# Two sums of an S5 step moved from VectorE to GpSimd, and the scan placed two places later

## The chip, the core and the metric

The kernel runs on one core of a Trainium2 chip. Its engines are TensorE (PE in the profile, its weight loads PEld), VectorE (DVE), ScalarE (ACT), GpSimd (POOL) and SyncE (SP); 16 DMA engines move the data. Each engine has its own list of instructions and runs it in order, and the lists meet in semaphores. The metric is the device time of one execution in microseconds; lower is better.

## The reference

A two-layer decoder trunk over 256 tokens of 1024 channels in float32. Layer 0: RMSNorm and a mixer of dilated attention and a gating unit. Layer 1: RMSNorm, then an S5 layer and a sigmoid GLU. Behind each mixer stands a PEER layer: for each token and each of 8 heads, 16 of 16384 experts are chosen, and an expert is a row u and a row v of 1024 channels each:

```python
act = jax.nn.gelu(jnp.einsum('td,tkd->tk', xbb, u_tab[ib]))
return jnp.einsum('tk,tkd->td', gb * act, v_tab[ib])
```

The S5 layer is a complex diagonal recurrence along time. For each state, with input x (real part xr, imaginary xi) and a fixed complex factor a of size `dec` and angle `th`, it computes s[k] = a s[k-1] + x[k], and the output is the real part of a product with c, plus a skip.

## The kernel before

**The frame.** The 256 tokens are two halves t = 0, 1 of 128 (one on each partition). Two layers by two halves by 8 heads by 16 experts make 512 *places* g. For each place GpSimd issues one gather (L463) that brings u and v rows for 128 tokens, 1 MB, into one of nine ring buffers. VectorE takes the dot of u with the token (`dot_product`, L1324, 128x1024, both operands in SBUF). ScalarE makes gelu, weight and a diagonal matrix (`weights`, L661 to L667), and TensorE multiplies the diagonal by v (`expert`, L920), which adds to a sum in PSUM. The gather of place g waits for the expert matmuls of place g - 9, since it takes their buffer.

**The rest of the work** hangs between the places. A table WORK, written by hand in `between()`, names for each place what else is done there. Each engine goes through the same table and takes the stages that it has a function for. On VectorE the stages of a place come before its dot; on ScalarE before its weights; on TensorE before the expert matmuls of the place ahead. So a stage at place p waits on each engine for that engine's work of the places before.

**S5.** The first half's S5 layer runs in the places behind 128, the second's in those behind 256. Each goes through eight steps c = 0 to 7 of 128 channels (512 states, 4 columns of 128 times per part), nine places apart: slot = 11 + 9c. To keep the recurrence real, the input is turned by the angle of its time, scanned with the real factor, and turned back. The stages of step (t, c):

- s5_turns (ScalarE, L591 and L593, at slot + 3 of the step before): the turns for each time, and `whole`, the rounded turns
- s5_frac (VectorE, L1186, at slot + 4 of the step before): waits for `whole`, leaves the fraction
- s5_tables (ScalarE, at slot + 6 of the step before): cosine and sine tables
- s5_in (TensorE): the input in PSUM
- s5_rot (VectorE, L1213 and L1214, slot + 1): input by cosine and by sine, 128x1024 each, from PSUM and a table; then w_ok
- s5_add (VectorE, L1218 and L1219, slot + 2): the two sums, 128x512 each; in the second half also the start value (L1223)
- s5_scan (VectorE, L1231 twice, slot + 3), and in the first half a copy of the last column (L1235)
- s5_cmat (ScalarE, L629 and L631, slot + 4)
- s5_back (VectorE, L1240 and L1242, slot + 5): two products 128x1024
- s5_out (TensorE, L882 and L886, slot + 6): waits for both products; then yc_done, for which the next s5_rot waits

The choice of the experts of later heads (`route_...`) also runs on VectorE in between, mostly with operations of one input.

Of the kernel before, what the change touches and what calls it, by code (L numbers as in the profile page):

```python
# [19 lines left out]
ALU = mybir.AluOpType  # L20
# [9 lines left out]
KC = D // P  # L30
# [3 lines left out]
PH, NK, TOPK = 8, 128, 16  # L34
EXPERTS = NK * NK
GROUPS = 2 * T * PH
RING = 9
AHEAD = 16
PACE = 1
DIAGS = 16  # L40
# [54 lines left out]
def between():  # L95

    work = {n: {} for n in range(GROUPS)}

    def at(n, slot, *stages):
        work[n + slot // TOPK].setdefault(slot % TOPK, []).extend(stages)  # L100

    def query(n, slot, phase, b):
        at(n, slot, ("q_mm", phase, b, 0, 3))
        at(n, slot + 1, ("q_mm", phase, b, 3, 6))
        at(n, slot + 2, ("q_mm", phase, b, 6, 8))
        at(n, slot + 3, ("q_in", phase, b))
        at(n, slot + 4, ("q_turn", phase, b))
        at(n, slot + 6, ("q_copy", phase, b))
        at(n, slot + 7, ("q_score", phase, b))
        at(n, slot + 9, ("q_keep", phase, b))  # L110

    def norm(n, slot, m):
        for i, name in enumerate(("norm_sq", "norm_ms", "norm_sd", "norm_h", "norm_T", "hT_copy")):
            if m < 8 or i < 4:
                at(n, slot + i, (name, m))

    def mix_norm(n, slot, m):
        for i, name in enumerate(("norm_sq", "norm_ms", "norm_sd", "norm_r", "norm_d", "norm_T", "hT_copy")):
            at(n, slot + i, (name, m))

    def product(n, slot, name, *which):
        at(n, slot, (name, *which, 0, 3))
        at(n, slot + 1, (name, *which, 3, 6))
        at(n, slot + 2, (name, *which, 6, 8))

    def attention(n, slot, a):
        for i, name in enumerate(("att_scores", "att_max", "att_exp", "att_den", "att_pT", "att_pT_copy", "att_o")):
            at(n, slot + i, (name, a))

    at(0, 0, ("z_out", 6), ("z", 7, 0, 8), ("z", 8, 0, 8), ("z", 9, 0, 8), ("z_out", 7), ("z_out", 8), ("z_out", 9))  # L130
    at(0, 2, ("qk_turn", 1))
    at(0, 3, ("qkT_copy", 1))
    query(0, 6, 0, 1)
    at(1, 1, ("sgu_var", 1))
    at(1, 2, ("sgu_sd", 1))
    at(1, 3, ("sgu_norm", 1))
    at(1, 4, ("sgu_mm", 1))
    at(1, 5, ("sgu_gate", 1))
    attention(1, 6, 1)
    query(1, 13, 0, 2)  # L140
    attention(2, 6, 2)
    at(2, 14, ("mix", 1))
    at(2, 15, ("mix_T", 1))
    at(3, 0, ("mixT_copy", 1))
    product(3, 1, "w_mm", 1, 0)
    at(3, 4, ("w_sum", 1, 0))
    product(3, 4, "w_mm", 1, 1)
    at(3, 7, ("w_sum", 1, 1))
    norm(3, 8, 3)
    query(3, 14, 0, 3)  # L150
    query(4, 4, 1, 3)
    for slot, *names in ((78, "s5_dt"), (79, "s5_th"), (80, "s5_dec"), (81, "s5_n"), (82, "s5_trig"), (84, "s5_k"),
                         (86, "s5_b0"), (90, "s5_b1"), (106, "s5_bT"), (108, "s5_bT_copy")):
        at(0, slot, (names[0],))
    query(0, 76, 1, 0)
    query(0, 84, 1, 1)
    query(0, 92, 1, 2)
    for t in range(T):
        g = PH * (t + 1)
        at(g, 2, ("y_sum", 2 + 2 * t))  # L160
        mix_norm(g, 3, 4 + 2 * t)
        at(g, 3, ("s5_turns", t, 0))
        at(g, 4, ("s5_frac", t, 0))
        at(g, 6, ("s5_tables", t, 0))
        for c in range(KC):
            slot = 11 + 9 * c
            at(g, slot - 1 if c == 0 else slot - 6, ("s5_in", t, c))
            at(g, slot, ("s5_decay", t, c))
            at(g, slot + 1, ("s5_rot", t, c))
            at(g, slot + 2, ("s5_add", t, c))  # L170
            at(g, slot + 3, ("s5_scan", t, c))
            at(g, slot + 4, ("s5_cmat", t, c))
            at(g, slot + 5, ("s5_back", t, c))
            if c + 1 < KC:
                at(g, slot + 3, ("s5_turns", t, c + 1))
                at(g, slot + 4, ("s5_frac", t, c + 1))
                at(g, slot + 6, ("s5_tables", t, c + 1))
            at(g, slot + 6, ("s5_out", t, c))
            if c % 4 == 3:
                at(g, slot + 8, ("s5_gelu", t, c // 4))  # L180
        for b in range(2):
            at(g, 82 + 2 * b, ("glu_mm", t, b, 0, 4))
            at(g, 83 + 2 * b, ("glu_mm", t, b, 4, 8), ("gate_T", t, b))
            at(g, 86 + 2 * b, ("glu_sig", t, b))
            at(g, 87 + 2 * b, ("glu_sum", t, b))
        norm(g, 90, 5 + 2 * t)
        for b in range(4):
            query(g, 96 + 6 * b, 2 + t, b)
    at(24, 2, ("y_sum", 6))
    norm(24, 3, 8)  # L190
    for n, slot in ROUTE_AT.items():
        for name, i in ROUTE:
            at(0, slot + i, (name, n))
    return work


WORK = between()

LAST = [("y_sum", 7), ("norm_sq", 9), ("norm_ms", 9), ("norm_sd", 9), ("norm_h", 9)]
# [6 lines left out]
def trunk(nc, x_in, vecs, cols_in, cst_in, w_in, sgu_g, sgu_wT, sgu_bT, w_out, s5_par, s5_b, s5_c, glu_w, wq, skT, uv_tab,  # L206
          out):
    with ExitStack() as ctx:
# [3 lines left out]
        def sem(name):  # L212
            return ctx.enter_context(nc.semaphore(name))
# [46 lines left out]
        def part(start, size, pattern="p (a s) -> p a s", **dims):  # L260
# [43 lines left out]
        by_cos, by_sin = (part(5888 + 1024 * v, 1024, "p (r j s) -> p r j s", r=2, j=4) for v in range(2))  # L304
# [14 lines left out]
        ld_vec, ld_col, ld_row = sem("ld_vec"), sem("ld_col"), sem("ld_row")  # L319
        got = [sem(f"got{b}") for b in range(RING)]  # L320

        r_ok, rd_ok, sn_done, dt5_ok, dd_ok = (sem(n) for n in ("r_ok", "rd_ok", "sn_done", "dt5_ok", "dd_ok"))
        sq_done, ms_done, sd_done, h_done, nT_done, hT_act, hT_dve, x_done, w_used = (sem(n) for n in (
            "sq_done", "ms_done", "sd_done", "h_done", "nT_done", "hT_act", "hT_dve", "x_done", "w_used"))

# [122 lines left out]
        @block.gpsimd  # L448
        def _(pool):
            pool.wait_ge(ld_sgu, 48)  # L450
            sg3 = sgw[:, :].rearrange("p (h i) -> p h i", h=8)
            nc.gpsimd.affine_select(out=sg3, in_=sg3, pattern=[[0, 8], [1, P]], compare_op=ALU.is_ge, fill=0.0, base=0,
                                    channel_multiplier=-1).then_inc(sgm_ok, 1)

            for g in range(GROUPS * TOPK):
                n, s = g // TOPK, g % TOPK
                if s == 0:
                    pool.wait_ge(idx_ok, n + 1)
                if g < RING and g % 2 == 0:
                    pool.wait_ge(z_done, 6 + g // 2)  # L460
                if g >= RING:
                    pool.wait_ge(v_done, g - RING + 1)
                nc.gpsimd.indirect_dma_start(  # L463
                    out=ring[g % RING], out_offset=None, in_=uv_tab,
                    in_offset=bass.IndirectOffsetOnAxis(ap=idx[n % AHEAD][:, s:s + 1], axis=0)).then_inc(got[g % RING], 16)

# [478 lines left out]
        def _(dve):  # L945
            V = nc.vector
# [267 lines left out]
                V.tensor_tensor(by_sin, x4, sin, ALU.mult).then_inc(w_ok, 1)  # L1214
                dve.drain()

            def s5_add(t, c):
                V.tensor_tensor(by_cos[:, 0, :, :], by_cos[:, 0, :, :], by_sin[:, 1, :, :], ALU.add)  # L1218
                V.tensor_tensor(by_cos[:, 1, :, :], by_cos[:, 1, :, :], by_sin[:, 0, :, :], ALU.subtract)  # L1219
                dve.drain()  # L1220
                if t == 1:

                    V.tensor_tensor(by_cos[:, :, :, 0], by_cos[:, :, :, 0], z_last[:, :, 4 * c:4 * c + 4], ALU.add)  # L1223
                    dve.drain()

            def s5_scan(t, c):

                dve.wait_ge(dt5_ok, KC * t + c + 1)
                for r in range(2):
                    w = by_cos[:, r, :, :].rearrange("p j s -> p (j s)")  # L1230
                    ins = V.tensor_tensor_scan(w, decay.rearrange("p j s -> p (j s)"), w, 0.0, ALU.mult, ALU.add)  # L1231
                ins.then_inc(sn_done, 1)
                dve.drain()
                if t == 0:
                    V.tensor_copy(z_last[:, :, 4 * c:4 * c + 4], by_cos[:, :, :, P - 1])  # L1235
# [83 lines left out]
            def dot_product(g):  # L1319
# [8 lines left out]
                         att_max=att_max, att_den=att_den, sgu_var=sgu_var, sgu_norm=sgu_norm, sgu_gate=sgu_gate, mix=mix,  # L1328
                         mixT_copy=mixT_copy, w_sum=w_sum, q_copy=q_copy, y_sum=y_sum, s5_n=s5_n, s5_k=s5_k,
                         s5_b0=s5_b0, s5_b1=s5_b1, s5_rot=s5_rot,  # L1330
                         s5_frac=s5_frac, s5_add=s5_add, s5_scan=s5_scan, s5_back=s5_back, glu_sum=glu_sum, norm_r=norm_r)
            stage |= dict(route_keys=route_keys, route_pairs=route_pairs, route_best=route_best, route_index=route_index,
                          route_gate=route_gate)

            def run(stages):
                for name, *args in stages:
                    if stage.get(name):
                        stage[name](*args)
# [82 lines left out]
```

## Time and profile before

| | |
|---|---|
| median of 3 runs | 1553.53 us (1551.04 to 1553.55) |
| the profiled execution, its own time | 1553.37 us |
| its span, first to last instruction | 1551.6 us |
| VectorE, ScalarE, GpSimd busy | 1111.5, 770.2, 589.4 us |
| TensorE matmuls, mean granted clock | 1097.8 us, 0.781 |
| gathers | 512, 84.8% of the DMA engines' span |

The 1.8 us between span and time lie around the first and the last instruction. Busy shares are means over stages with different limits, so they don't say what bounds a stage; the windows and the waits of a stretch do. A wait of an engine counts only where that engine sets the end.

### The profile page before, as it was taken

The page shows a single profiled execution, that of the slowest core. Times are in us where ns is not written, and L with a number is a line of the kernel's source. Part 1 is how long each engine was busy: PE and PEld are TensorE (multiplying, and loading weights), DVE is VectorE, ACT ScalarE, POOL GpSimd, SP SyncE. Part 2 cuts the span into 40 slices and gives each one's busy share as a digit, 9 for nine tenths or more (in the row PEclk, how much of TensorE's full clock was granted, in tenths as well). Part 3 has the DMA queues.
Part 4 walks back from the last instruction along what each step waited for, and adds up shares of the span by engine and source line. Part 5 has one row for each costly group of instructions (what it writes and reads, how often), then busy time and mean ns, then how long its engine had stood idle before and what let it go on. Part 6 is the DMA issues. An engine that isn't in the chain of part 4 may idle for free.

```text
span 1551.6 us, 19133 instructions
## 1 busy us (share of the span) xinstructions
PE 1097.8 (71%) x5920; PEld 348.4 (22%) x5920; DVE 1111.5 (72%) x2533; ACT 770.2 (50%) x2120; POOL 589.4 (38%) x517
## 2 busy tenths in 40 slices
PE   7997678866765666679866575656878666666665
PEld 3542222322211212223221121212323111111110
DVE  2356887479787899985477799999456866666554
ACT  2315554445456667764334666766334644444433
POOL 0024343323443354554334345344432443434430
PEclk9998689878966776879988567686998777676675
DMA  9569999999999998999999999999999999999995
GB/s 358 179 234 413 420 405 418 414 415 408 415 421 421 354 374 358 410 421 415 412 413 414 403 357 369 355 363 406 380 416 415 415 422 421 421 421 421 421 422 234
DMA packets 105418, 603.39 MB, mean 389 GB/s; under 512 B 9314, under 2 KB 9442, under 8 KB 39780
## 3 DMA queue, kind: packets, MB, share of 16 engines
q0 software_dynamic: 73728, 536.90, 84.8%
q1 hardware_dynamic: 31588, 65.26, 11.3%
q8 instruction: 47, 0.77, 0.2%
q14 instruction: 55, 0.45, 0.1%
HBM read 601.08 MB, written 1.05 MB: 388 GB/s over the span
## 4 chain that ended last, share of the span: by engine, by line
DMA 32%; DVE 31%; PE 22%; ACT 7%; issue 3%; DVEq 3%; ACTq 1%; POOL 1%; SPq 0%; POOLq 0%
DMA rings<-in_uv_tab_dram,idx 24%; DVE rings L1324 11%; PE ps L715 9%; PE ps L920 8%; DMA wst<-in_wq_dram 7%; DVE mem L1231 2%; PE ps L908 2%; DVE dgs L1324 2%; ACT dgs L667 1%; DVE mem L1213 1%; ACT wgt L664 1%; DMA rings<-in_w_in_dram 1%; DVE mem L1242 1%; ACT L661 1%; DVE mem L1240 1%
## 5 line engine op out<-in xcount | busy, mean ns | idle before, releaser
L920 PE MATMUL ps<-rings,dgs 64*64 64x512 f32 x3648 | 638.0, 804 | 343.3 <-ACT dgs L667 342.6
L463 POOL DMA_INDIRECT rings<-in_uv_tab_dram,idx x456 | 521.7, 1144 | 804.3 <-PE ps L920 687.8
L1324 DVE CUSTOM_DVE_ANT_0 rings<-rings,h 128x1024 f32<-128x1024 f32 x456 | 550.7, 1224 | 210.8 <-DMA rings<-in_uv_tab_dram,idx 197.7
L661 ACT ACTIVATE gel<-dots 128x1 f32<-128x1 f32 x512 | 102.1, 199 | 522.2 <-DVE dots L1324 518.5
L920 PEld LDWEIGHTS ps<-rings,dgs 64*64 64x64 f32 x3648 | 128.3, 163 | 783.4 <-ACT dgs L667 682.3
L667 ACT ACTIVATE dgs<-cst,wgt 128x128 f32<-128x128 f32 x512 | 205.6, 402 | 36.3 <-issue 1.5
L715 PE MATMUL ps<-wst,hT 128*128 128x512 f32 x320 | 168.0, 666 | 37.1 <-DMA wst<-in_wq_dram 20.5
L664 ACT ACTIVATE wgt<-gel,share 128x1 f32<-128x1 f32 x512 | 150.8, 295 | 35.5 <-issue 0.3
L920 PE MATMUL ps<-dgs 64*64 64x512 f32 x448 | 80.2, 795 | 53.2 <-ACT dgs L667 53.1
L463 POOL DMA_INDIRECT dgs<-in_uv_tab_dram,idx x56 | 65.9, 1176 | 88.3 <-PE ps L920 74.8
L715 PEld LDWEIGHTS ps<-wst,hT 128*128 128x128 f32 x320 | 63.4, 212 | 138.1 <-issue 134.9
L1324 DVE CUSTOM_DVE_ANT_0 dgs<-dgs,h 128x1024 f32<-128x1024 f32 x56 | 68.5, 1223 | 26.5 <-DMA dgs<-in_uv_tab_dram,idx 24.5
L661 ACT ACT_TABLE_LOAD x56 | 71.8, 1283 | 3.8 <-DVE dots L1324 2.2
L715 PE MATMUL ps<-rings,hT 128*128 128x512 f32 x128 | 59.0, 611 | 3.7 <-DMA rings<-in_w_in_dram 2.8
L1324 DVE DVE_READ_ACCUMULATOR2_ANT dots<- 128x1 f32 x512 | 42.6, 83 | 0.0
L648 ACT ACT_TABLE_LOAD x31 | 39.8, 1283 | 0.8
L920 PEld LDWEIGHTS ps<-dgs 64*64 64x64 f32 x448 | 14.2, 156 | 106.9 <-ACT dgs L667 101.2
L1231 DVE TENSOR_TENSOR_SCAN mem<-mem 128x512 f32<-128x512 f32 x32 | 37.4, 1210 | 0.0
L556 ACT ACTIVATE mem<-ps 128x512 f32<-128x512 f32 x16 | 9.5, 594 | 53.6 <-PE ps L715 53.6
L715 PEld LDWEIGHTS ps<-rings,hT 128*128 128x128 f32 x128 | 24.4, 197 | 33.2 <-issue 33.1
L1108 DVE COPY mem<-ps 128x512 f32<-128x512 f32 x16 | 11.0, 689 | 27.4 <-PE ps L707 27.4
L908 PE MATMUL ps<-wst,hT 128*128 128x512 f32 x64 | 29.6, 605 | 0.0
(192 smaller groups left out, 991.2 us busy)
## 6 DMA issues: line engine op xcount, KB each, us to landing
wst<-in_wq_dram SPq DMA_DIRECT2D x15, 2048.0 KB, 28.2
wst<-in_w_out_dram SPq DMA_DIRECT2D x4, 2048.0 KB, 22.8
wst<-in_glu_w_dram SPq DMA_DIRECT2D x4, 2048.0 KB, 31.7
rings<-in_uv_tab_dram,idx POOLq DMA_INDIRECT x456, 15.7
rings<-in_w_in_dram SPq DMA_DIRECT2D x3, 2048.0 KB, 16.7
rings<-in_w_in_dram SPq DMA_DIRECT2D x2, 1024.0 KB, 7.5
dgs<-in_w_in_dram SPq DMA_DIRECT2D x1, 2048.0 KB, 19.4
vec<-in_vecs_dram SPq DMA_DIRECT2D x3, 512.0 KB, 17.2
```

What stands on the lines that cost most here:

```text
L463: nc.gpsimd.indirect_dma_start(out=ring[g % RING], out_offset=None, in_=uv_tab, in_offset=bass.IndirectOffsetOnAxis(ap=idx[n % AHEAD][:, s ...
L648: A.activation(gexp[n % 2][:, :], cs[n % 2][:, :], ACT.Exp, bias=ncs[n % 2], accum_out=gsum[n % 2]).then_inc(exp_ok, 1)
L661: A.activation(gel[i][:, every], dots[i][:, every], ACT.Gelu_apprx_tanh)
L664: A.activation(wgt[i][:, c], gel[i][:, c], ACT.Copy, scale=share[n % AHEAD][:, c])
L667: A.activation(diag[:, (g + k) % DIAGS, :], ident, ACT.Copy, scale=wgt[i][:, c]).then_inc(diag_ok, 1)
L715: ins = PE.matmul(ps[:, bank, :], lhs[:, k, :], rhs[:, k, :], start=(k == 0), stop=(k == KC - 1))
L908: ins = PE.matmul(ps[:, 2 + b, :], hTs[t][:, k, :], wst[:, w % 2, k, :], start=False, stop=(k == KC - 1))
L920: ins = PE.matmul(ps[64 * b:64 * b + 64, 4 + 2 * t + half, :], diag[rows, g % DIAGS, rows], ring[g % RING][rows, D + b * BANK:D + (b + 1) ...
L1213: V.tensor_tensor(by_cos, x4, cos, ALU.mult)
L1231: ins = V.tensor_tensor_scan(w, decay.rearrange("p j s -> p (j s)"), w, 0.0, ALU.mult, ALU.add)
L1240: V.tensor_tensor(by_sin, by_cos, sin, ALU.mult).then_inc(d_ok, 1)
L1324: V.tensor_tensor_reduce(out=u, in0=u, in1=h[:, t, :], scale=1.0, scalar=0.0, op0=ALU.mult, op1=ALU.add, accum_out=dots[n % 2][:, s:s + 1] ...
```

## The change

The two sums of s5_add leave VectorE and go to GpSimd, between its gathers. GpSimd goes through the same table six places behind its gathers: ahead of the gather of place g it does the stages of place g - 6. It waits for w_ok ahead of the sums and raises add_ok behind them. On VectorE s5_scan waits for add_ok, and the addition of the start value moves into it. In the table the scan goes from slot + 3 to slot + 5 and s5_back from slot + 5 to slot + 6; s5_add stays at slot + 2, which counts for GpSimd alone.

```diff
+POOL_LAG = 6
...
-            at(g, slot + 3, ("s5_scan", t, c))
+            at(g, slot + 5, ("s5_scan", t, c))
             at(g, slot + 4, ("s5_cmat", t, c))
-            at(g, slot + 5, ("s5_back", t, c))
+            at(g, slot + 6, ("s5_back", t, c))
...
+            def s5_add(t, c):
+
+                pool.wait_ge(w_ok, KC * t + c + 1)
+                nc.gpsimd.tensor_tensor(by_cos[:, 0, :, :], by_cos[:, 0, :, :], by_sin[:, 1, :, :], ALU.add)
+                nc.gpsimd.tensor_tensor(by_cos[:, 1, :, :], by_cos[:, 1, :, :], by_sin[:, 0, :, :],
+                                        ALU.subtract).then_inc(add_ok, 1)
+
+            stage = dict(s5_add=s5_add)
+
+            def run(stages):
+                for name, *args in stages:
+                    if name in stage:
+                        stage[name](*args)
+
             for g in range(GROUPS * TOPK):
                 n, s = g // TOPK, g % TOPK
+                if g >= POOL_LAG:
+                    run(WORK[(g - POOL_LAG) // TOPK].get((g - POOL_LAG) % TOPK, []))
                 if s == 0:
                     pool.wait_ge(idx_ok, n + 1)
...
-            def s5_add(t, c):
-                V.tensor_tensor(by_cos[:, 0, :, :], by_cos[:, 0, :, :], by_sin[:, 1, :, :], ALU.add)
-                V.tensor_tensor(by_cos[:, 1, :, :], by_cos[:, 1, :, :], by_sin[:, 0, :, :], ALU.subtract)
-                dve.drain()
+            def s5_scan(t, c):
+
+                dve.wait_ge(add_ok, KC * t + c + 1)
                 if t == 1:
 
                     V.tensor_tensor(by_cos[:, :, :, 0], by_cos[:, :, :, 0], z_last[:, :, 4 * c:4 * c + 4], ALU.add)
                     dve.drain()
-
-            def s5_scan(t, c):
-
                 dve.wait_ge(dt5_ok, KC * t + c + 1)
```

## Rows read from the trace of the kernel before

**Rows 1.** The page: engines, and slices of VectorE, GpSimd and DMA.
```profile
PE 1097.8 (71%) x5920; PEld 348.4 (22%) x5920; DVE 1111.5 (72%) x2533; ACT 770.2 (50%) x2120; POOL 589.4 (38%) x517
...
DVE  2356887479787899985477799999456866666554
POOL 0024343323443354554334345344432443434430
...
GB/s 358 179 234 413 420 405 418 414 415 408 415 421 421 354 374 358 410 421 415 412 413 414 403 357 369 355 363 406 380 416 415 415 422 421 421 421 421 421 422 234
```
**Rows 2.** Windows: PE, PEld, DVE, ACT, POOL busy; clock, DMA share, GB/s.
```profile
520.00:640.00 120.00, 74.44 (x586) 24.33 (x586) 114.36 (x217) 82.12 (x227) 55.35 (x42) 0.73 0.93 363
640.00:680.00 40.00, 27.54 (x244) 9.52 (x244) 36.39 (x55) 31.08 (x91) 21.89 (x18) 0.81 1.01 421
...
880.00:1080.00 200.00, 125.86 (x911) 38.41 (x912) 189.49 (x377) 132.72 (x365) 92.38 (x71) 0.71 0.94 369
...
1120.00:1500.00 380.00, 260.90 (x1284) 58.45 (x1280) 249.57 (x593) 162.18 (x484) 154.42 (x147) 0.74 1.01 419
```
**Rows 3.** VectorE's waits in 880 to 1080 us: total, times, longest.
```profile
DVE tiny L1315 <- ACT gexp L648: 1.2, 1, 1.2
DVE cand L1304 <- issue: 0.4, 1, 0.4
```
**Rows 4.** VectorE's waits in 1120 to 1500 us.
```profile
DVE rings L1324 <- DMA rings<-in_uv_tab_dram,idx: 99.5, 81, 2.0
DVE dgs L1324 <- DMA dgs<-in_uv_tab_dram,idx: 16.4, 12, 2.5
```
**Rows 5.** Timeline of VectorE at step (1,2): start, length, line, tiles.
```profile
937.20 1.22 DVE L1214 TENSOR_TENSOR mem<-ps,mem 128x1024 f32<-128x1024 f32 x1
...
939.70 0.69 DVE L1218 TENSOR_TENSOR mem<-mem 128x512 f32<-128x512 f32 x1
940.30 0.69 DVE L1219 TENSOR_TENSOR mem<-mem 128x512 f32<-128x512 f32 x1
941.06 0.18 DVE L1223 TENSOR_TENSOR mem<-mem,z_last 128x8 f32<-128x8 f32 x1
941.35 1.23 DVE L1324 CUSTOM_DVE_ANT_0 dgs<-dgs,h 128x1024 f32<-128x1024 f32 x1
942.50 0.08 DVE L1324 DVE_READ_ACCUMULATOR2_ANT dots<- 128x1 f32 x1
942.50 2.34 DVE L1231 TENSOR_TENSOR_SCAN mem<-mem 128x512 f32<-128x512 f32 x2
944.97 1.23 DVE L1324 CUSTOM_DVE_ANT_0 rings<-rings,h 128x1024 f32<-128x1024 f32 x1
...
946.12 0.69 DVE L1186 SCALAR_TENSOR_TENSOR mem<-mem 128x512 f32<-128x512 f32 x1
...
947.87 1.22 DVE L1240 TENSOR_TENSOR mem<-mem 128x1024 f32<-128x1024 f32 x1
949.18 1.23 DVE L1242 TENSOR_TENSOR mem<-mem 128x1024 f32<-128x1024 f32 x1
950.32 1.22 DVE L1324 CUSTOM_DVE_ANT_0 rings<-rings,h 128x1024 f32<-128x1024 f32 x1
```
**Rows 6.** Timeline of ScalarE at the same step.
```profile
943.25 0.40 ACT L667 ACTIVATE dgs<-cst,wgt 128x128 f32<-128x128 f32 x1
943.56 1.26 ACT L591 ACTIVATE mem<-cst,s5s 128x128 f32<-128x128 f32 x4
944.89 0.63 ACT L593 ACTIVATE mem<-mem 128x512 f32<-128x512 f32 x1
```
**Rows 7.** Timeline of VectorE at step (1,6): route_keys ahead of s5_frac.
```profile
1043.84 0.49 DVE L1262 MAX8 top<-scr 128x8 f32<-128x128 f32 x2
...
1045.65 1.23 DVE L1324 CUSTOM_DVE_ANT_0 rings<-rings,h 128x1024 f32<-128x1024 f32 x1
```
**Rows 8.** Timeline of GpSimd at step (1,2).
```profile
939.75 1.44 POOL L463 DMA_INDIRECT rings<-in_uv_tab_dram,idx  x1 [0.77 <-PE ps L920]
941.50 1.89 POOL L463 DMA_INDIRECT rings<-in_uv_tab_dram,idx  x1 [0.30 <-PE ps L920]
```
**Rows 9.** Timeline of GpSimd at step (1,0).
```profile
882.04 1.84 POOL L463 DMA_INDIRECT rings<-in_uv_tab_dram,idx  x1 [0.30 <-issue]
886.63 0.94 POOL L463 DMA_INDIRECT rings<-in_uv_tab_dram,idx  x1 [2.74 <-PE ps L920]
```
**Rows 10.** Timeline of VectorE at step (1,0).
```profile
886.35 1.22 DVE L1214 TENSOR_TENSOR mem<-ps,mem 128x1024 f32<-128x1024 f32 x1
```
**Rows 11.** Groups of GpSimd's instructions: count, busy us, mean ns.
```profile
L452 POOL TENSOR_SCALAR_AFFINE_SELECT sgw<-sgw 128x1024 f32<-128x1024 f32 x1 | 1.6, 1593 | 37.5 <-DMA sgb<-in_sgu_bT_dram 37.5
```

More of the change, by code:

```diff
@@ L322, in trunk @@
         r_ok, rd_ok, sn_done, dt5_ok, dd_ok = (sem(n) for n in ("r_ok", "rd_ok", "sn_done", "dt5_ok", "dd_ok"))
+        add_ok = sem("add_ok")
         sq_done, ms_done, sd_done, h_done, nT_done, hT_act, hT_dve, x_done, w_used = (sem(n) for n in (
@@ L1330, in _ @@
                          s5_b0=s5_b0, s5_b1=s5_b1, s5_rot=s5_rot,
-                         s5_frac=s5_frac, s5_add=s5_add, s5_scan=s5_scan, s5_back=s5_back, glu_sum=glu_sum, norm_r=norm_r)
+                         s5_frac=s5_frac, s5_scan=s5_scan, s5_back=s5_back, glu_sum=glu_sum, norm_r=norm_r)
             stage |= dict(route_keys=route_keys, route_pairs=route_pairs, route_best=route_best, route_index=route_index,
```

## The prediction

> **What bounds the kernel now.** I read the page first [rows 1]: VectorE is busy 72% and GpSimd 38% of the span, but the slices say more than the shares. For most of the run the DMA engines are full and move about 415 to 421 GB/s; they fall to 354 to 374 in two places, slices 14 to 16 and 24 to 27, and there VectorE shows 8 and 9 tenths. The windows sharpen this [rows 2]: in 520 to 640 us (S5 of the first 128 tokens) 363 GB/s with VectorE busy 114.36 of 120; in 880 to 1080 us (second 128 tokens) 369 GB/s and 189.49 of 200; outside, 419 to 421 GB/s. The list of waits confirms who leads. In 880 to 1080 us VectorE waits 1.6 us in all, none of it for a gather [rows 3]; in 1120 to 1500 us it waits for gathers 81 + 12 times, 115.9 us [rows 4]. So in the S5 stretches VectorE is the bound and each microsecond put on it or taken off it moves the end; elsewhere the gathers are, and VectorE time is free. What is gained or lost in a VectorE stretch stays to the end, because the full DMA stretch behind it only starts earlier or later. The DMA loss in both stretches is the most that could ever be won: (420-363)/420 x 120 = 16 us and (420-369)/420 x 200 = 24 us.
>
> From about 640 us the DMA is full again [rows 2] although S5 of the first half goes on to about 690. Gathers are asked for nine places before they are used, so what VectorE gains after some 615 us of the first half buys only waiting. I count there the S5 steps c = 0 to 3, and in the second half all eight: 12 of 16.
>
> **Adds taken from VectorE.** The two sums take 0.69 us each but are pipelined; from the first to what follows them it is 939.70 to 941.06, or 1.36 us [rows 5]; with the drain ahead of the next dot, 1.4. Over 12 steps, -16.8 us. Over all 16 it would be 22.
>
> **The scan moved from slot + 3 to slot + 5.** This looks free, the same work in another order. It is not, because of what stood behind the scan. At slot + 4 VectorE does s5_frac (L1186), which needs `whole` from ScalarE (L593). ScalarE starts that work at slot + 3 behind the weights of place slot + 2, which need its dot. In the step shown the dot of slot + 2 is in the accumulator at 942.58; ScalarE does gelu, weight and diagonal to 943.65, the four turns and `whole` to 944.89 + 0.63 = 945.52, that is 2.94 us after the dot [rows 6]. VectorE came to s5_frac at 946.12, 3.54 us after the dot, because two scans (942.50 to 944.97, 2.47 us) and one dot (1.15) lay between [rows 5]. The wait was hidden by 0.6 us. Take the scans out and VectorE is there 1.15 us after the dot and stands 1.8 us. Then the scans are still to be done. Per step: -1.4 (sums) - 0.6 (s5_frac sooner) + 2.47 (scans elsewhere) = +0.5 us. I found the same distance, 2.94 to 3.07, at all 14 steps that prepare a next one from behind a scan; VectorE came at 3.54 to 3.58 in 12 of them. Two have other work in the gap: at (0,0) a route_gate makes it 3.96, the step costs only +0.1; at (1,6) route_keys (1043.84 to 1045.6, 1.8 us) lies between [rows 7], together with the dot 2.97 us, which covers the wait: -1.4. Step c = 7 prepares nothing: -1.4. First half: 0.1 + 3 x 0.5 = +1.6. Second: 6 x 0.5 - 1.4 - 1.4 = +0.2. Together +1.8 us. The wait takes the gain away, before any cost on GpSimd.
>
> **s5_back from slot + 5 to slot + 6.** The same two products; but TensorE's s5_out, in the same place, now waits for them ahead of the expert matmuls of slot + 5, which come some 2.6 us later (two products, 2.45 us [rows 5], less the dot's and ScalarE's part, plus the S5 matmuls). The gather nine places on is issued that much later. Cover: in the stretch VectorE never waits for a gather [rows 3]; price nothing. I keep +2 us as the upper bound, for the end of the first half where the DMA is full again.
>
> **The sums on GpSimd.** Queued behind them there: the gather of slot + 8 and later. The wait for w_ok is short: at 12 steps the gather ahead of the sums was issued 0 to 5 us after the second product (L1214) had ended (step (1,2): product to 938.42, gather 939.75 + 1.44 [rows 5, 8]); in two it was 3.7 to 3.9 us earlier ((1,0): gather to 883.88 [rows 9], product to 887.57 [rows 10]). Two come within 0.3 us of its end before it. The scan at slot + 5 comes 7 us after the products at the soonest, so add_ok is there.
>
> How long is one sum on GpSimd? The trace has none. The nearest row is the select over 128x1024 with one input, 1.59 us [rows 11]. By elements written a sum of 512 would be half, 0.8; by elements read, 1.6. I take 1.2, and keep 0.8 and 1.6.
>
> What does VectorE do meanwhile? The gathers show that the two engines share something. A gather issue that begins while VectorE has an operation with two operands in SBUF stands until that has ended: 939.75 begins in L1218 (939.70 to 940.39) and takes 1.44; 941.50 begins in a dot (941.35 to 942.58) and takes 1.89 [rows 5, 8]. The issue of 886.63 begins in L1214, whose one input is in PSUM, and takes 0.94 [rows 9, 10]. Nearly all issue times beyond 0.94 fit "0.94 + what was left of VectorE's operation", and an issue gets in even between two dots back to back. A gather only reads its index, so it does not show the other direction. A sum reads for its whole time. I take it that VectorE's next operation with two SBUF operands (dot, scan, s5_frac, s5_back) then stands. The Trainium skill says so outright (SBUF — State Buffer, Who interferes with whom): such a VectorE instruction contends with a GpSimd one that reads SBUF, and the second to issue fully blocks; this trace agrees for GpSimd as the second, and no row shows VectorE as the second. For the length, the skill's GPSIMD Engine Reference (3.1, Elementwise) gives about 2.6 cycles an element at 1.2 GHz, an estimate of 1.1 us; with it the sum below would be 1.8 + 6 x 1.65 + 5 x 0.4 = 13.7 us in place of 15.6.
>
> Price of it, by where the sums fall. *Late* (GpSimd free 2.2 to 4 us after the products; five steps, (0,1), (0,3), (1,1), (1,2), (1,4)): the first sum falls behind dot slot + 2, then a dot, then the second sum: 1.2 + 1.15 + 1.2 = 3.55 from that dot, where VectorE stands to 2.95 anyway: +0.6 each, +3.0. (1,3) has route_best, of one-input operations, over it: 0. *Early* (free at the products or with no wait behind it to hide in: (0,0), (0,2), (1,0), (1,5), (1,6), (1,7)): one block of 1.2 surely, the second half the time: 1.8 each, +10.8.
>
> **Sum.** +1.8 + 3.0 + 10.8 = +15.6 us on the profiled 1553.37: 1569.0. That run lies 0.16 us under the median of the three, so nothing is added.
>
> **Rivals.**
> (a) *The wait alone*: GpSimd gives way and VectorE runs on. +1.8 us: 1555.2, range 1551 to 1558. For it: no dot in the trace is longer than 1.23 us although issues overlap with them [rows 5]. Against it: issues do stand behind VectorE, so the two are not independent.
> (b) *Faster*, the other side: the stand at s5_frac isn't there. The place is one, slot + 4, and it decides: the gain is 1.4 less (2.95 less VectorE's work between the dot of slot + 2 and s5_frac). With 1.15 us of work it is a loss, from 1.55 us on a gain, from 2.95 the full 1.4. All twelve steps covered: -16.8, 1536.6. For it, route work like that of (1,6) fills gaps; against it, only two steps of 14 have it, and the order is fixed.
> (c) *Starved queue*: sums and their own waits, some 3.6 us a step, hold the gathers so that DMA becomes late too, or add_ok comes after the scan's place. GpSimd is busy 92.38 of 200 us there [rows 2], which speaks against it; were it so, 3.6 - 1.2 us more a step, +29 on top: about 1595.
>
> **Chances.** Wait and block 0.56; (a) 0.27, of which 0.21 within 0.2% (3.1 us, about what a measurement of this kernel can tell from no change); (b) 0.12; (c) 0.05. Faster 0.12, same 0.21, slower 0.56 + 0.06 + 0.05 = 0.67. The likeliest case's own range: at 0.8 us a sum, early 6 x 1.2 and late 0: +9, 1562; at 1.6, early all twice 6 x 3.2, late 5 x 1.4, +28, 1581. The range over all, with (b) left out below and (c) above: 1551 to 1580.
>
> **What would show it.** In the profile after: s5_frac with idle time of 1.5 to 1.9 us from ScalarE's L593 (now L611 or so) at 12 steps; dots and scans beside the sums lengthened to over 2 us; GpSimd sums of about 1.2 us each; VectorE's waits for gathers still near none in 880 to 1080 us; add_ok never waited for. I am wrong if s5_frac shows no idle time, if dots stay at 1.22 (then (a)), or if VectorE waits for gathers or sums (then (c)).

## The result and the profile after

The changed kernel takes 1574.45 us (median of 4 runs, 1573.85 to 1575.32) against 1553.54 us before (1551.04 to 1554.68): ratio 1.0137, interval 1.012 to 1.0155, +20.9 us. The profiled execution took 1574.22 us with a span of 1572.5. Slower, within the range, 5 us above the forecast.

The page after, the same lines as in [rows 1]:

```profile
PE 1099.2 (70%) x5920; PEld 346.5 (22%) x5920; DVE 1117.8 (71%) x2501; ACT 770.2 (49%) x2120; POOL 635.8 (40%) x549
...
GB/s 358 186 236 417 421 410 417 414 416 411 415 422 410 326 348 346 391 421 413 414 413 415 356 384 331 326 342 372 396 415 417 421 422 420 421 421 421 421 421 222
```

VectorE has 32 instructions fewer, the sums, but is busy 6.3 us more. The DMA dips are in the same place and deeper. The windows of the two stretches, to be read against [rows 2]:

```profile
520.00:640.00 120.00, 71.67 (x536) 22.26 (x536) 108.08 (x198) 76.77 (x216) 63.29 (x51) 0.71 0.89 337
...
880.00:1080.00 200.00, 121.46 (x914) 39.78 (x918) 177.27 (x343) 126.32 (x348) 100.10 (x79) 0.70 0.90 346
```

363 and 369 GB/s became 337 and 346; in 1120 to 1500 us it is 419 as before. VectorE now has idle time in the stretch; its waits in 880 to 1090 us, against [rows 3]:

```profile
DVE mem L1204 <- ACT mem L611: 10.0, 6, 1.8
DVE hT L997 <- PE ps L761: 4.9, 1, 4.9
DVE idx L1322 <- issue: 0.4, 1, 0.4
```

L1204 is s5_frac, L611 ScalarE's `whole`. (The wait at L997 is the next norm, reached because the window is 10 us longer.) There is none for a gather and none for add_ok. In 520 to 640 us the same wait is 7.7 us in 5 times.

One S5 step, (1,0), on VectorE. L1232 is the second product, L1338 the dot, L1204 s5_frac, L1245 the scan:

```profile
894.60 1.22 DVE L1232 TENSOR_TENSOR mem<-ps,mem 128x1024 f32<-128x1024 f32 x1
895.91 0.16 DVE L1329 RECIPROCAL tiny<-tiny 128x1 f32<-128x1 f32 x1
896.15 1.04 DVE L1331 TENSOR_SCALAR share<-gexp,tiny 128x16 f32<-128x16 f32 x1
897.10 1.21 DVE L1338 CUSTOM_DVE_ANT_0 rings<-rings,h 128x1024 f32<-128x1024 f32 x1
898.25 0.08 DVE L1338 DVE_READ_ACCUMULATOR2_ANT dots<- 128x1 f32 x1
898.25 2.27 DVE L1338 CUSTOM_DVE_ANT_0 dgs<-dgs,h 128x1024 f32<-128x1024 f32 x1
900.45 0.08 DVE L1338 DVE_READ_ACCUMULATOR2_ANT dots<- 128x1 f32 x1
900.45 1.22 DVE L1338 CUSTOM_DVE_ANT_0 rings<-rings,h 128x1024 f32<-128x1024 f32 x1
901.59 0.08 DVE L1338 DVE_READ_ACCUMULATOR2_ANT dots<- 128x1 f32 x1
903.50 0.69 DVE L1204 SCALAR_TENSOR_TENSOR mem<-mem 128x512 f32<-128x512 f32 x1 [1.82 <-ACT mem L611]
904.11 1.22 DVE L1338 CUSTOM_DVE_ANT_0 rings<-rings,h 128x1024 f32<-128x1024 f32 x1
905.25 0.08 DVE L1338 DVE_READ_ACCUMULATOR2_ANT dots<- 128x1 f32 x1
905.25 0.17 DVE L1240 TENSOR_TENSOR mem<-mem,z_last 128x8 f32<-128x8 f32 x1
905.49 2.34 DVE L1245 TENSOR_TENSOR_SCAN mem<-mem 128x512 f32<-128x512 f32 x2
```

GpSimd beside it, and ScalarE's `whole`, each from the timeline of its engine:

```profile
895.90 1.26 POOL L460 TENSOR_TENSOR mem<-mem 128x512 f32<-128x512 f32 x1 [3.77 <-DVE mem L1232]
897.12 2.32 POOL L461 TENSOR_TENSOR mem<-mem 128x512 f32<-128x512 f32 x1
899.59 1.76 POOL L481 DMA_INDIRECT rings<-in_uv_tab_dram,idx  x1
```
```profile
902.84 0.63 ACT L611 ACTIVATE mem<-mem 128x512 f32<-128x512 f32 x1
```

Read them against each other. The first sum runs from 895.90 to 897.16, undisturbed, 1.26 us. VectorE's tensor_scalar of 896.15, 16 elements and 0.23 us elsewhere, stands until 897.19. Then the dot of 897.10 has the memory first, and the second sum stands until 898.3; it takes 2.32 us. It is now in front of the dot of 898.25, which takes 2.27 and not 1.22. So in this step the engines take turns, an instruction at a time, and each sum caught costs VectorE 0.8 to 1.05 us. Last, VectorE has nothing between the dots and s5_frac and stands 1.82 us: 903.50 less 900.53, the end of the dot of slot + 2, is 2.97. To the next step's products it is 24.5 us, before 22.1: +2.4 us, of it 0.8 + 1.05 for the blocks and 0.5 for the order. The first products of this step and of the next, after:

```profile
893.47 1.22 DVE L1231 TENSOR_TENSOR mem<-ps,mem 128x1024 f32<-128x1024 f32 x1
917.97 1.22 DVE L1231 TENSOR_TENSOR mem<-ps,mem 128x1024 f32<-128x1024 f32 x1
```

and before, with the tensor_scalar at its usual length:

```profile
885.22 1.22 DVE L1213 TENSOR_TENSOR mem<-ps,mem 128x1024 f32<-128x1024 f32 x1
887.90 0.23 DVE L1317 TENSOR_SCALAR share<-gexp,tiny 128x16 f32<-128x16 f32 x1
907.35 1.22 DVE L1213 TENSOR_TENSOR mem<-ps,mem 128x1024 f32<-128x1024 f32 x1
```

They don't always take turns. At step (1,2) both sums go ahead of one dot, though its record starts 0.1 us before the first sum's; the dot stands for both:

```profile
949.85 3.67 DVE L1338 CUSTOM_DVE_ANT_0 rings<-rings,h 128x1024 f32<-128x1024 f32 x1
```
```profile
949.95 1.27 POOL L460 TENSOR_TENSOR mem<-mem 128x512 f32<-128x512 f32 x1
951.16 1.26 POOL L461 TENSOR_TENSOR mem<-mem 128x512 f32<-128x512 f32 x1
```

Each VectorE operation's length, less the median of the same operation in the trace of before (where it is 0.12 us or more), adds up beside the sums to 19.2 us in the 12 steps that the prediction counts, and to 25.9 us in all 16.

### The profile page after: what moved, and what is told of

Same layout as the page of the kernel before. It is cut to its first block, busy times and chain, and to the rows that moved or that the text cites. A ratio compares the mean times of both kernels' runs of the same rounds, so it can differ in the third digit from the quotient of the medians.

```text
span 1572.5 us, 19125 instructions
## 1 busy us (share of the span) xinstructions
PE 1099.2 (70%) x5920; PEld 346.5 (22%) x5920; DVE 1117.8 (71%) x2501; ACT 770.2 (49%) x2120; POOL 635.8 (40%) x549
## 3 DMA queue, kind: packets, MB, share of 16 engines
HBM read 601.08 MB, written 1.05 MB: 383 GB/s over the span
## 4 chain that ended last, share of the span: by engine, by line
DMA 31%; DVE 29%; PE 22%; ACT 8%; DVEq 4%; issue 3%; POOL 1%; ACTq 1%; SPq 0%; POOLq 0%
DMA rings<-in_uv_tab_dram,idx 24%; DVE rings L1338 11%; PE ps L733 10%; PE ps L938 7%; DMA wst<-in_wq_dram 4%; DMA dgs<-in_uv_tab_dram,idx 2%; PE ps L926 2%; DVE mem L1245 2%; ACT dgs L685 1%; DVE dgs L1338 1%; DVEq L1247 1%; DVE mem L1256 1%; ACT wgt L682 1%; DVE mem L1254 1%; POOL rings L481 1%
## 5 line engine op out<-in xcount | busy, mean ns | idle before, releaser
L938 PE MATMUL ps<-rings,dgs 64*64 64x512 f32 x3648 | 627.6, 787 | 330.6 <-ACT dgs L685 329.5
L1338 DVE CUSTOM_DVE_ANT_0 rings<-rings,h 128x1024 f32<-128x1024 f32 x456 | 567.8, 1261 | 216.2 <-DMA rings<-in_uv_tab_dram,idx 203.6
L938 PEld LDWEIGHTS ps<-rings,dgs 64*64 64x64 f32 x3648 | 122.0, 160 | 770.6 <-ACT dgs L685 692.5
L733 PE MATMUL ps<-wst,hT 128*128 128x512 f32 x320 | 168.6, 668 | 23.5 <-ACT scr L584 15.0
L938 PE MATMUL ps<-dgs 64*64 64x512 f32 x448 | 85.5, 846 | 47.2 <-ACT dgs L685 47.2
L1338 DVE CUSTOM_DVE_ANT_0 dgs<-dgs,h 128x1024 f32<-128x1024 f32 x56 | 70.6, 1260 | 28.4 <-DMA dgs<-in_uv_tab_dram,idx 26.9
L900 PE MATMUL ps<-hT,one_diag 128*128 128x128 f32 x32 | 11.6, 460 | 52.7 <-DVE mem L1256 52.7
L1338 DVE DVE_READ_ACCUMULATOR2_ANT dots<- 128x1 f32 x512 | 42.1, 82 | 0.0
L1245 DVE TENSOR_TENSOR_SCAN mem<-mem 128x512 f32<-128x512 f32 x32 | 37.4, 1210 | 0.6
L904 PE MATMUL ps<-mem 128*32 128x128 f32 x512 | 30.7, 417 | 0.0
## 6 DMA issues: line engine op xcount, KB each, us to landing
rings<-in_uv_tab_dram,idx POOLq DMA_INDIRECT x456, 16.2
dgs<-in_w_in_dram SPq DMA_DIRECT2D x1, 2048.0 KB, 19.4
```

Of the source, the lines that this page charges most:

```text
L733: ins = PE.matmul(ps[:, bank, :], lhs[:, k, :], rhs[:, k, :], start=(k == 0), stop=(k == KC - 1))
L904: ins = PE.matmul(ps[32 * j:32 * j + 32, bank, cols_], m[:, j, v, :], z_[:, r, j, :], start=False, stop=(q == 3))
L938: ins = PE.matmul(ps[64 * b:64 * b + 64, 4 + 2 * t + half, :], diag[rows, g % DIAGS, rows], ring[g % RING][rows, D + b * BANK:D + (b + 1) ...
L1338: V.tensor_tensor_reduce(out=u, in0=u, in1=h[:, t, :], scale=1.0, scalar=0.0, op0=ALU.mult, op1=ALU.add, accum_out=dots[n % 2][:, s:s + 1] ...
```

## The experiments

Each ratio is against the kernel before, run on the same chip.

**1. The order alone.** The sums stay on VectorE.

```diff
-            at(g, slot + 3, ("s5_scan", t, c))
+            at(g, slot + 5, ("s5_scan", t, c))
-            at(g, slot + 5, ("s5_back", t, c))
+            at(g, slot + 6, ("s5_back", t, c))
```

> The kernel before with the new places alone: scan at slot + 5, s5_back at slot + 6, the two sums still on VectorE. My theory, the stand at s5_frac: per step the scans' 2.47 us come back later and only 0.6 us of them is saved at s5_frac, so +1.9 us at (0,1) to (0,3) and (1,0) to (1,5), +1.5 at (0,0), nothing at (1,6) and at c = 7: 9 x 1.9 + 1.5 = +18.6 us on the kernel before, about 1572; s5_frac waits some 1.8 us for ScalarE in about 11 steps. Rival, all the loss is GpSimd's: no change, 1553.5.

1571.48 us, ratio 1.012 (1.0105 to 1.0135): +18.2 us. VectorE's group of s5_frac in 500 to 1100 us (count, busy, mean ns, idle before and for whom); before, the two idle times of this line were 3.4 us in the whole run, both at the first steps:

```profile
L1186 DVE SCALAR_TENSOR_TENSOR mem<-mem 128x512 f32<-128x512 f32 x15 | 10.4, 692 | 25.2 <-ACT mem L593 25.2
```

Moving the scan and s5_back, with nothing added, costs nearly as much as the whole change. Run 2 moves s5_back alone, and between it and this run lies the scan's move alone: 1571.48 - 1548.81 = +22.7 us, of which a gain of s5_back hides 4.5. The expected 18.6 was for the scan's move with s5_back at no price, so it was 4 us short, and that 18.2 came so close is in part luck. One reason for the 4 us is probably the count of steps: the DMA engines move 372 GB/s in 640 to 660 us here, 422 before, so VectorE still sets the time in a step of the first half that was not counted.

**2. s5_back alone** at slot + 6, the scan at slot + 3.

> The kernel before with s5_back alone at slot + 6. My theory: the expert matmuls of slot + 5 come later, but VectorE never waits for that gather: 0, between -1 and +1 us. Rival, TensorE's delay reaches the gathers and the end: +2 us or more.

1548.81 us, ratio 0.9968 (0.9956 to 0.9979): -4.5 us. Both expectations were wrong; this part of the change makes the kernel faster. The trace shows one reason. VectorE's route_gate waits for ScalarE's exponential (L1315 on L648), in the whole run, before and in this run:

```profile
  ACT gexp L648: 4.7, 3
```
```profile
  ACT gexp L648: 2.4, 1
```

Two waits of 1.2 us, one in each S5 stretch, are gone: 2.3 of the 3.0 us by which the spans differ. s5_back now stands behind the dot of slot + 5 and not ahead of it. ScalarE's tables and the exponential behind them come after the weights that need this dot, so against VectorE they are sooner: in the stretch of the second half the exponential starts at 932.96 and the operation that waits for it at 933.39 before; here at 928.62 and 930.24, with no wait. The rest I did not pin down.

**3. s5_frac one place later**, all else as changed.

```diff
-                at(g, slot + 4, ("s5_frac", t, c + 1))
+                at(g, slot + 5, ("s5_frac", t, c + 1))
```

> The changed kernel with s5_frac one place later, at slot + 5 ahead of the scan. ScalarE's whole is then there. Theory of two losses: the stand (17.7 us over the two stretches in the trace after) goes, the blocks by GpSimd's reads stay and those that hid in the stand now show (about +2): 1574.5 - 17.7 + 2 = about 1559. Rival, the block alone explains the loss and the stand only took its place: 1570 or more. Rival, GpSimd costs nothing at all: 1536 to 1540.

1555.09 us, ratio 1.0014 (1.0005 to 1.0023). That is 19.4 us less than the changed kernel, for one number in a table. The idle time at s5_frac in 500 to 1100 us fell from 20.2 to 2.4 us, and the blocks stayed; the dots in that window still average over 1300 ns against 1223 before:

```profile
L1338 DVE CUSTOM_DVE_ANT_0 rings<-rings,h 128x1024 f32<-128x1024 f32 x187 | 240.2, 1307 | 50.7 <-DMA rings<-in_uv_tab_dram,idx 45.6 <-issue 0.5
...
L1204 DVE SCALAR_TENSOR_TENSOR mem<-mem 128x512 f32<-128x512 f32 x15 | 10.3, 690 | 2.4 <-ACT mem L611 1.7
```

**4. No sums at all**, on neither engine (the run leaves out the two sums), otherwise as 3.

```diff
-            stage = dict(s5_add=s5_add)
+            stage = dict()
...
-                dve.wait_ge(add_ok, KC * t + c + 1)
```

> The changed kernel with s5_frac at slot + 5, and the two sums left out altogether, on both engines (the scan reads the products as they are). What is left is the time without sums and without blocks. Theory: before, less the sums 16.8 us, less what s5_back at slot + 6 gave (4.7): about 1532; the difference to the same kernel with the sums on GpSimd (1555.1) is then the price of the blocks, about 23 us. Rival, the kernel is bound elsewhere too and GpSimd's price is smaller: 1540 or more.

1532.62 us, ratio 0.9866 (0.9849 to 0.9882), as expected. Between this and run 3 lie only GpSimd's sums and VectorE's wait for them, for which the trace of 3 has no idle time: their price is 1555.1 - 1532.6 = 22.5 us (the kernel before differs by 0.4 us between the chips of the two runs). In the trace of 3 VectorE's operations beside the sums are longer than before by 19.4 us in the 12 steps counted and 25.1 us in all 16. Run 2 less this run is 16.2 us, about what the sums cost on VectorE; but run 2 also has the scan at slot + 3 and s5_frac at slot + 4, and no run separates that. GpSimd takes more from VectorE than it gives.

**5. Reads on GpSimd beside an unchanged VectorE.**

```diff
+                for k, op in enumerate((ALU.add, ALU.subtract)):
+                    if 2 * (KC * t + c) + k:
+                        pool.wait_ge(spare_ok, 2 * (KC * t + c) + k)
+                    nc.gpsimd.tensor_tensor(spare[:, :], cst[:, 128:640], cst[:, 256:768],
+                                            op).then_inc(spare_ok, 1)
```

> The kernel before, all of its work where it was, and beside it on GpSimd, six gathers ahead, two additional sums of 128x512 per S5 step that read constants and write a spare buffer nobody reads. VectorE's list is unchanged. Theory of the block by reads: VectorE's operations with two SBUF operands stand about 1.05 us for each sum that is caught, 1 to 2 per step, 12 steps that count: +13 to +22 us, 1567 to 1575, with dots and scans of about 2.3 us in the trace. Rival, GpSimd gives way: 0, dots at 1.22. Rival, the gathers are held and starve VectorE: slower with waits of VectorE for gathers in 880 to 1080 us.

1581.37 us, ratio 1.0183 (1.0168 to 1.0197): +28 us, more than expected, with no wait of VectorE for a gather in 880 to 1080 us. VectorE's operations beside the sums are longer by 23.8 us in the 12 steps counted and by 31.9 in all 16. Data that nobody uses slow VectorE down, so it is not the dependence on the sums. At step (1,2), VectorE:

```profile
958.74 1.47 DVE L1244 TENSOR_TENSOR mem<-mem,z_last 128x8 f32<-128x8 f32 x1
960.33 2.27 DVE L1345 CUSTOM_DVE_ANT_0 dgs<-dgs,h 128x1024 f32<-128x1024 f32 x1
```

and GpSimd:

```profile
958.90 2.62 POOL L464 TENSOR_TENSOR spare<-cst 128x512 f32<-128x512 f32 x2
```

An addition of 8 elements, 0.18 us in [rows 5], takes 1.47: it ends 0.05 us after the first sum would (958.90 + 1.26).

**6. Writes on GpSimd** at the same points: four memsets of 128x512 in place of the sums.

```diff
+                for k in range(4):
+                    if 4 * (KC * t + c) + k:
+                        pool.wait_ge(spare_ok, 4 * (KC * t + c) + k)
+                    nc.gpsimd.memset(spare[:, :], 0.0).then_inc(spare_ok, 1)
```

> The kernel before, and on GpSimd, at the same points as in the run with additional reads, four memsets of 128x512 into a spare buffer: writes and no reads. Theory of the block by reads: VectorE is left alone, 0, 1552 to 1555, dots at 1.22. Rival, any work of GpSimd in memory blocks VectorE, or holding the gathers up costs by itself: +10 us or more.

1555.89 us, ratio 1.0016 (1.0007 to 1.0025), +3.0 us between the medians. GpSimd and VectorE at step (1,2):

```profile
943.50 2.29 POOL L464 MEMSET spare<- 128x512 f32 x4
```
```profile
943.36 0.17 DVE L1243 TENSOR_TENSOR mem<-mem,z_last 128x8 f32<-128x8 f32 x1
943.65 1.22 DVE L1344 CUSTOM_DVE_ANT_0 dgs<-dgs,h 128x1024 f32<-128x1024 f32 x1
```

The same engine is held nearly as long at the same point (2.29 us, and 2.62 in run 5) and the dot beside it has its 1.22 us. For dots, scans and additions it is the reads. Not for every operation: at step (0,0) two tensor_scalars of 16 elements beside the memsets take 0.52 and 0.45 us, in the trace of before 0.21 and 0.19 in the mean. The 3.0 us are about the most that holding the gathers up 2.3 us a step costs; I did not separate them further.

**7. The sums one gather later**, POOL_LAG = 7.

> The changed kernel with the sums seven gathers behind in place of six, so some 2.5 us later beside VectorE. If a block falls behind the dot of slot + 2 it hides in the stand at s5_frac. Theory: in most of the steps that were early the second block hides: 6 x 0.8 = 5 us less, about 1569.5. Rival, the sums are then late for the scan: VectorE waits for add_ok, 1575 or more. Rival, where the block falls makes no difference: 1574.5.

1574.31 us, ratio 1.0139 (1.0121 to 1.0156): no change, the third expectation. The sums did come later at most steps of the first half, but not at (1,0), (1,3), (1,5) and (1,7), where they still begin as the products end. Where both fell into the stand, at (1,4), no dot is longer, yet the step is not shorter: s5_frac itself was then behind the sum, and took 1.93 us for 0.69. My notion that the stand could hide the block at will fell here.

**8. The sums on TensorE.** GpSimd has only its gathers. Identity times product, added up in PSUM; the scan reads PSUM.

```diff
+            def s5_add(t, c):
+
+                pe.wait_ge(w_ok, KC * t + c + 1)
+                for r in range(2):
+                    PE.matmul(ps[:, r, :], ident, by_cos[:, r, :, :], start=True, stop=False)
+                    ins = PE.matmul(ps[:, r, :], minus[:, :] if r else ident, by_sin[:, 1 - r, :, :], start=False, stop=True)
+                ins.then_inc(add_ok, 1)
```

> The two sums on TensorE: identity and minus identity times the products, added up in PSUM, four matmuls of 128x512 a step at slot + 2; the scan reads PSUM, at slot + 4, s5_frac at slot + 5, s5_back at slot + 6, the next s5_in at slot + 7 of the step. TensorE shares nothing with VectorE and is busy 126 of 200 us there. Theory: before - 16.8 (sums) - 4.7 (s5_back) = 1532, up to 1536 for the matmuls in front of the experts'. Rival, the four matmuls (0.6 to 0.8 us each) make the scan or the gathers late: 1545 or more, with waits of VectorE for TensorE at the scan.

1540.8 us, ratio 0.9916 (0.9901 to 0.9932). Faster than before, 5 to 9 us over what I expected. In 500 to 1090 us VectorE waits for TensorE at s5_in (L871), which now shares its part of PSUM with the sums and waits for the scan before it, and at the sums (L880), in two places:

```profile
DVE mem L1223 <- PE ps L871: 6.0, 6, 1.3
...
DVE mem L1238 <- PE ps L880: 5.5, 5, 1.3
DVE ps L1233 <- PE ps L880: 3.2, 3, 1.9
```

**9 and 10. Two other orders for it.** In 9 the scan is at slot + 5 and the next s5_in at slot + 6, ahead of s5_out; in 10 the scan stays at slot + 4 and s5_in is at slot + 5.

> The sums on TensorE with the scan at slot + 5 in place of slot + 4, and the next s5_in at slot + 6, ahead of s5_out. VectorE waited 8.7 us for TensorE's sums and 6.0 us for s5_in in the two S5 stretches of the run with the sums on TensorE (1540.8). Theory: both waits go, the rest is the time without sums, 1532.6: 1533 to 1536. Rival, the waits only move to s5_out and the gathers: 1540 or more.

> The sums on TensorE, scan at slot + 4 as in the first such run, with s5_in at slot + 5 of the step before in place of slot + 7. Theory: the 6.0 us of waits for s5_in go, the 8.7 us for the sums stay: about 1536 to 1538. Rival, s5_in there holds TensorE up for VectorE's scan and the experts come later: 1540 or more.

9: 1537.15 us, ratio 0.9886 (0.9872 to 0.9901), -17 us, the fastest version here that does all the work, and 1 us above what was expected. Its waits for the sums are down from 8.7 to 3.6 us and those for s5_in are gone. TensorE's granted clock in 880 to 1080 us is 0.86 here and 0.71 before; whether that gives a part of the gain, no run separates. 10: 1540.1 us, ratio 0.9917 (0.9902 to 0.9931), no better than 8, its rival's time: the waits for s5_in are gone, and those for the sums have grown from 8.7 to 12.7 us.

## Why the prediction was right

**What bounds.** Right: no wait of VectorE for a gather in 880 to 1080 us, in any version with slower VectorE work, and each change of its work came through to the end.

**Sums taken away, -16.8 us**: 16.2 (4 against 2, with the other places of scan and s5_frac in the difference).

**The scan's new place.** Right in mechanism, short in size. Forecast +1.8 with the sums gone, which is +18.6 without that gain. The order alone measured +18.2, but that contains s5_back's gain; the scan's move by itself is +22.7 (1 against 2). Removing the stand (3) gave back 19.4. At s5_frac the trace shows 1.82 us where 1.8 was forecast, 17.7 us in 11 times in the two stretches.

**s5_back, "price nothing".** Wrong in sign of what was left open: -4.5 us. I had looked only at who waits for s5_back, not at what the dot that now goes ahead of it releases on ScalarE, and so which wait of VectorE falls away.

**GpSimd's sums.** The mechanism was right, in the direction that no row of before showed. The length was right too, 1.26 us against 1.2. The term was mis-sized: "+3.0" late and "+10.8" early, 13.8 together, where changed kernel against order alone gives 16.8 + (1574.45 - 1571.48) = 19.8, and 22.5 with the stand away. The trace after shows where, by how much VectorE's operations are lengthened. The early term held: its six steps have 10.2 us against 10.8. A block was shorter than the 1.2 I took, 0.8 to 1.1 us, but the second sum was caught in five of the six, where I gave it half. The late term did not: its five steps have 7.2 us, of which 0.9 hid in the stand, so 6.3 against 3.0. GpSimd had its gathers out sooner than in the trace of before, so three of them, (0,3), (1,1) and (1,2), began within 0.3 us of the products' end and had nothing to hide in. And (1,3), priced at 0 for its one-input operations, has 1.8 us: the dot, and a tensor_scalar with one tensor and a constant, 0.88 us for 0.16.

**The sum.** By runs: -4.5 (s5_back) - 16.2 (sums) + 22.5 (blocks) + 19.4 (stand) = +21.2, measured +20.9. These are differences of neighbours in one chain of runs from the kernel before to the changed one, so that they add up is no test of the parts. By the forecast's own terms: scan and sums +1.8, by runs 22.7 - 16.2 = +6.5; s5_back 0, by runs -4.5; GpSimd's sums +13.8, by runs +19.2 with 16.2 for the sums. The first two misses, +4.7 and -4.5, cancel by luck; what is left of the error of 5 us is mostly the late steps and (1,3).

**Rivals.** (a), GpSimd gives way, is refuted by 5; (b), no stand, by 1; (c), starved queue, by the absence of waits, and 6 bounds it at 3.0 us. (Its time, 1595, should be 1598 by its own terms, 1569 + 29; nothing rests on it.)

## What to carry to other kernels

When an operation is moved out from between two waits, look up what wait it was covering: here two scans hid a stand of 1.8 us by 0.6 us, and one table entry was worth 19 us. GpSimd's elementwise work with SBUF inputs is no free second VectorE: beside a VectorE that is the bound and reads two operands from SBUF, it cost more than it took over; TensorE, with an identity and PSUM, was the engine with room. Before a work-splitting change is timed, time it with the moved work left out: run 4 showed at once what there was to win and what the new place cost.

## What the runs showed of the hardware

- GpSimd's sum of 128x512 with both inputs in SBUF takes 1.26 us undisturbed, up to 2.3 behind a dot; VectorE's takes 0.69. The estimate worked out in the prediction from the Trainium skill (GPSIMD Engine Reference, 3.1) was 1.1 us.
- VectorE's operations with two SBUF operands stand for the rest of a sum on GpSimd: 2.27 for 1.22 us, 1.47 for 0.18. This is the half of the Trainium skill's rule (SBUF — State Buffer, Who interferes with whom) that no row of before showed, and the traces of the change and of run 5 agree with it.
- By the starts of the records alone one can't tell who stands: the dot of 3.67 us starts 0.10 us, and the addition of 1.47 us starts 0.16 us, before the sum that it stands for.
- A tensor_scalar stands too, with a scalar operand from SBUF (1.04 for 0.23 us) and with a constant (0.88 for 0.16). At step (1,1) MAX8 and FIND_INDEX8 beside the second sum keep their usual length, 0.48 us for two and 0.28.
- Memsets on GpSimd, 2.29 us for four, leave dots and additions of VectorE at their usual length; two tensor_scalars beside them took 0.52 and 0.45 us for about 0.2.
